# Two transfers of the bias strips moved one head earlier in the gated-attention stage

## The reference, cut to what matters

```
z = hn @ w_in                       # queries, keys, values, gate, rank-16 gate input
la = log_sigmoid(a @ w_gate2 + b_gate) / 16
for each block of 64 tokens:        # per head
    o = qd @ s + tril(qd @ kd.T) @ v
    s = s * exp(b_last) + (k * exp(b_last - b)).T @ v
o = rmsnorm(o) * norm_g ; out = (o * silu(g)) @ w_out
```

```
idx = clip(offset + a - j, -128, 128) + 128
bias = table[:, idx]                # 16 heads x 257 distances
```

## Time and profile before

| | |
|---|---|
| Median of 3 runs | 3154.01 us (3152.77 to 3159.4) |
| Profiled execution, its own time | 3159.74 us |
| Profiled execution, span | 3158.0 us |
| TensorE busy | 2886.5 us, 91% of the span |
| Mean granted TensorE clock | 0.949 of full speed |
| DMA | 284.42 MB, 29.4% of 16 engines' span |
| Transfers of the strips | 4 of 1,536 KB, issued at 96.7, 167.9, 241.0 and 318.8 us |

### The profile page before, as it was taken

One profiled execution on the slowest core, in us unless ns is written; L12 is line 12 of the kernel. 1 busy time (PEld: TensorE's weight loads), 2 busy tenths in 40 slices (PEclk: granted clock), 3 DMA queues, 4 the chain that ended last, 5 costly groups with the idle time before them and its releaser, 6 DMA issues. The chain is left out here.

```text
span 3158.0 us, 48949 instructions
## 1 busy us (share of the span) xinstructions
PE 2886.5 (91%) x19644; PEld 2705.7 (86%) x19644; DVE 1293.0 (41%) x2442; ACT 980.4 (31%) x1884; POOL 959.2 (30%) x672
## 2 busy tenths in 40 slices
PE   6994998887999999999799999987969999999997
PEld 4884886777999999999788787866959999999996
DVE  5231333237555554211423433343185656551114
ACT  4432343213223233110333434353133222222102
POOL 1121111225344446441311212101154434346410
PEclk8997999878999999999899999998979999999998
DMA  5233311512222225320413433336112222234211
GB/s 163 56 66 62 81 38 59 188 74 64 72 80 68 81 67 183 114 70 26 145 58 90 133 94 108 90 109 207 51 54 84 73 75 77 71 130 157 91 35 60
DMA packets 328257, 284.42 MB, mean 90 GB/s; under 512 B 24385, under 2 KB 311121, under 8 KB 327265
## 3 DMA queue, kind: packets, MB, share of 16 engines
q1 hardware_dynamic: 328032, 281.29, 29.4%
HBM read 205.99 MB, written 90.96 MB: 94 GB/s over the span
## 5 line engine op out<-in xcount | busy, mean ns | idle before, releaser
L83 PE MATMUL f_ps<-f_x_hi,f_w_hi 128*128 128x288 f32 (+1 forms) x2976 | 932.5, 313 | 60.2 <-POOL f_x_lo L741 29.7
L84 PE MATMUL f_ps<-f_x_hi,f_w_lo 128*128 128x288 f32 (+1 forms) x2976 | 927.9, 312 | 0.0
L85 PE MATMUL f_ps<-f_x_lo,f_w_hi 128*128 128x288 f32 (+1 forms) x2976 | 925.9, 311 | 0.0
L83 PEld LDWEIGHTS f_ps<-f_x_hi,f_w_hi 128*128 128x128 f32 x2976 | 565.4, 190 | 67.4 <-issue 24.6
L85 PEld LDWEIGHTS f_ps<-f_x_lo,f_w_hi 128*128 128x128 f32 x2976 | 567.4, 191 | 0.0
L84 PEld LDWEIGHTS f_ps<-f_x_hi,f_w_lo 128*128 128x128 f32 x2976 | 566.3, 190 | 0.0
L728 POOL TENSOR_TENSOR f_w_lo<-f_w_whole,f_w_hi 128x512 fp32r<-128x512 f32 x136 | 188.5, 1395 | 392.5 <-DVE f_w_whole L980 172.5
L1057 DVE TENSOR_TENSOR res<-res,f_ps 128x384 f32<-128x384 f32 x192 | 106.5, 554 | 458.3 <-PE f_ps L85 458.3
L1003 DVE TENSOR_TENSOR res<-f_ps,res 128x288 f32<-128x288 f32 x308 | 140.3, 458 | 208.9 <-PE f_ps L85 199.3
L1003 DVE TENSOR_TENSOR f<-f_ps,f 128x288 f32<-128x288 f32 x308 | 139.9, 458 | 159.6 <-PE f_ps L85 150.3
L733 POOL TENSOR_TENSOR f_w_lo<-f_raw,f_w_hi 128x768 fp32r<-128x768 f32 (+1 forms) x64 | 109.2, 1707 | 269.6 <-ACT f_w_hi L856 269.6
(11 more groups left out here) (320 smaller groups left out, 5697.5 us busy)
## 6 DMA issues: line engine op xcount, KB each, us to landing
f_x_whole<-hid_rows SPq DMA_DIRECT2D x44, 576.0 KB, 4.5
res_rows<-res SPq DMA_DIRECT2D x4, 4608.0 KB, 16.0
res<-res_rows SPq DMA_DIRECT2D x32, 576.0 KB, 8.2
f_raw<-in_ffn_w_down SPq DMA_DIRECT2D x48, 384.0 KB, 3.4
hid_rows<-f SPq DMA_DIRECT2D x44, 288.0 KB, 2.5
hid_rows<-res SPq DMA_DIRECT2D x44, 288.0 KB
mix_w_stage<-in_gla_w_in SPq DMA_DIRECT2D x24, 512.0 KB, 4.1
f_raw<-in_ffn_w_gate SPq DMA_DIRECT2D x22, 512.0 KB, 4.0
```

What stands on the lines that cost most here:

```text
L83: pe.matmul(out, w_hi, x_hi, start=first, stop=False)
L84: pe.matmul(out, w_lo, x_hi, start=False, stop=False)
L85: return pe.matmul(out, w_hi, x_lo, start=False, stop=last)
```

## The change

In the first head both issues of `keep_strips` become two: parts 0 and 1 go out at the end of tile 0, parts 2 and 3 at the end of tile 3. In the second head none is left.

```
--- before.py
+++ after.py
@@ -1361,8 +1361,9 @@
                         for kind in "vg":
                             for c in range(2):
                                 fetch((kind, h + 1, c))
-                    if h < 2 and i in (0, NG):
-                        keep_strips(sp, S, 2 * h + i // NG)
+                    if h == 0 and i in (0, NG):
+                        for n in range(2):
+                            keep_strips(sp, S, 2 * i // NG + n)
                 send_states(H - 1)
                 for i in range(NT):
                     send_mixed((H - 1) * NT + i)
```

## The result

The changed kernel takes 3228.3 us (median of 4 runs, 3224.0 to 3235.7), the kernel before beside it 3156.7 (4 runs). The ratio is 1.023, 95% interval 1.0207 to 1.0254: 65 to 80 us slower. The profiled execution has a span of 3233.7 us against 3158.0, 75.7 more; the medians lie 71.6 apart. The forecast was 3229 and +75.

What follows compares the result with a forecast made beforehand. TensorE, busy 91% of the span, was taken as the bound; +62.9 (first pair), +53.6 (second pair) and -41.8 (hole removed) give +74.7 us, so 3229 on the median, range 3203 to 3246.

Steps and rivals of the forecast that it cites:

- What bounds the kernel, and the hole: TensorE, busy 91%; in the mixer's second head it waits behind part 2 of the strips; removing that gives -41.8 us.
- the recovery of the clock: Second stall: TensorE's clock recovers inside the wait for `mixed`; were it not, 1.9 us more.
- The first pair: First head, slot 4: part 1 behind part 0 lands values' first weights 61 us later; +62.9 us with the clock.
- The 1.85 for the clock: Slower slot after the second head's long wait, taken as the price of any long idle of TensorE: 1.85 us.
- The step taken on trust: Both parts of a pair use the same four engines; the second adds 61 us, bounds 0 to 61.
- The second pair: Parts 2 and 3, issued in the first head, delay next keys' weights and the first `mixed` transfers: +53.6 us.
- The held issue: SyncE's issue of part 1 may be held, as an earlier issue was for 14.69 us, but ends long before 222.
- worse than the sum: SyncE held at part 3, later fetches and `mixed` transfers bunch: 10 to 20 us more, 3240 to 3250; chance 0.03.
- The total: Whole kernel: 62.9 + 53.6 - 41.8 = +74.7 us on the span of 3158.0; 3229 on the median.
- The formula of the rivals: Change in time is 2x - 47.4 us, x being what the second part adds to 61; turns at 23.7.
- Side by side: The second part of a pair goes to four other engines and adds nothing, hole gone: 3112 us; chance 0.09.
- Overlap on the same engines: Two strip rows in flight share the gap, the second part adding 30 to 50 us: 3167 to 3207; chance 0.06.

Runs made afterwards that it cites:

- one part per gap: Kernel before with four single parts, part 2 moved to tile 3 of the second head and part 3 to tile 3 of the third: 3110.5 us, ratio 0.986.
- half second parts: Changed kernel with each pair's second transfer writing 64 of 128 copies, the other halves sent alone in later heads: 3165.9 us, ratio 1.0039 to the kernel before.
- merged pairs: Changed kernel with the two parts of each pair made one transfer of eight heads: 3111.2 us, ratio 0.9865 to the kernel before.

## Why the prediction was right

- *What bounds the kernel, and the hole.* Right. The hole is part 2 ahead of the `mixed` transfers, shown by one part per gap. Its size was 1.4 us too small: 78.17 minus 35.0 (four kernels without it) is 43.2, not 41.8. The yardstick was off, not the mechanism: slot 20 of the kernel before, which the earlier trace rows give as 13.28, takes 11.73 to 11.75 in all nine other kernels. In the kernel before, the clock granted in the window 404:408 is 0.70 and in 408:412 it is 0.88, with TensorE busy all through both and for 3.26 of the 4 us ahead of them; in the other nine it is 1.00 through that slot, after the same work. In the changed kernel only 40.5 of the 43.2 show, since slot 11 now carries the recovery of the clock after the second stall: it is 0.50 in 368:372, with TensorE busy throughout.
- *The first pair.* Right: +62.9 forecast, +62.0 measured, and the landing at 222.0 against 222.5. That the chain from values' weights to TensorE has no slack is shown by the half second parts, which cost 31.2 for 30.5. The 1.85 for the clock was not isolated: the rounding starts 60.4 us later and slot 4 grows by 62.0. The step taken on trust, that both parts use the same four engines, is shown by the share of 0.24 in the changed kernel together with the merged pairs.
- *The second pair.* Right in mechanism; that the sum agrees to the tenth (+53.6 forecast and measured) is luck, since two small errors cancel: the `mixed` copy starts at 364.10 and not 366.3, and the recovery of the clock, put inside that wait, is not all hidden: TensorE still has its clock at 0.50 in the window 358:360. It stands 46.1 and then 4.0 us, 50.1 in all, where 50 to 57 were named; the rest of the 53.6 is work at the lower clock between and behind the two waits.
- *The held issue.* Foreseen as harmless, and so it is: 25 and 22 us. That the fetches behind are held too, for longer, was named only under "worse than the sum"; no cost of it shows beyond their place in the queue: the states' load went out at 357.90, ahead of the forecast 360.5.
- *The total.* The terms came out as +62.0, +53.6 and -40.5 for +62.9, +53.6 and -41.8, so the errors of the first and the last cancel in part. The median of 3228.3 lies closer to 3229 than the forecast's working warrants: the medians differ by 71.6 and the profiled executions by 75.7.
- *The formula of the rivals.* The change in time as 2x - 47.4 gives +13.6 at half the bytes; measured were 8 to 17. Its turning point, a pair done in 85 us, was not tried, but the kernel that reads from DRAM, with a pair done in 30, lies far on the other side of it and gains.
- *Side by side* did not happen between the two transfers of a pair (share 0.24); it did inside one of eight heads (0.48), at the forecast time. *Overlap on the same engines* did not happen within SyncE's queue (26 GB/s in 110:135); between the queues of SyncE and ScalarE it did (52 GB/s in 236:240). *Worse than the sum* did not come.

## What to carry to other kernels

A transfer whose outermost dimension was 4, 8 or 16 ran on as many engines here (shares 0.24, 0.48 and 0.95), and the weights behind it in the queue landed only when it was through: 25.3 us after their issue behind one part, 86.1 behind two. Look at the DMA share of your own kernel, and where it stands at a fraction for long, try more in the outermost dimension before moving the transfer about; here the same pairs cost 2.3% as two transfers of four heads and gained 1.35% as one of eight. Before a second transfer is put behind a first, find what is issued next and what waits for it: here the reader already waited 3.55 us for the fetch, there was no slack, and 61 us in the queue were 62 us of the kernel. Here four other forms of the same 6 MB (one transfer, two of eight heads, one small one per gap, or a source in DRAM) all gave 3107 to 3111 us.

## What the runs showed of the hardware

A broadcast from one SBUF partition per engine moved 26 GB/s on four engines (share 0.24), 52 on eight (0.48), 104 on sixteen (0.95); the same broadcast from DRAM moved 104 on four. In the kernel before, the fetch of weights issued behind one such part at 136.20 brought the share to 0.86 (195 GB/s) in 137:139, then it was 0.23 (25 GB/s) in 141:143, and in 160:161, just before the landing at 161.5, 97 GB/s moved at 0.27: the last of the weights, on about four engines. Two queues of the same engines moved 52 GB/s on four engines (share 0.26) when each held such rows, twice the rate of one queue; but with rows of 1,024 bytes in the one and of 3,072 in the other they moved 33 GB/s, 34 rows of the one and 32 of the other in 4 us, so a second queue did not free the weights, which ScalarE rounded at 176.63 where it did at 161.58.
